# The first modulation by pairs of chunks, with four tiles of the first projection open at once

## What is computed

```
m = silu(cond) @ ada_w + ada_b          # cond: one row for context, one for latent tokens
shift, scale, ... = split(m, 6)         # six parts of 1024 columns; a second block has six more
h = rms_norm(x, norm1_g) * (1 + scale) + shift
z = h @ ab_w_in                         # 3088 columns; the first projection
qkv = silu(depthwise_conv3(z[qkv part]))   # 1536 columns, three taps along the tokens
```

## Time and profile before

| | |
|---|---|
| median of the runs | 1631.31 us |
| the profiled execution | 1633.56 us, its span 1631.7 us |
| TensorE busy | 1535.8 us (94%) |
| VectorE busy | 1126.5 us (69%) |
| ScalarE busy | 797.4 us (49%) |
| GpSimd busy | 122.9 us (8%) |
| data moved | 230.80 MB, 141 GB/s in the mean |

### The profile page before, as it was taken

The page is one execution under the profiler, slowest core; times in us unless marked ns, Lnnn a source line. Parts: engine busy times, 40 slices in busy tenths (PEclk is TensorE's granted clock), DMA queues, the critical chain, the costliest instruction groups (busy, mean ns, idle before and its releaser), DMA issues.

```text
span 1631.7 us, 31148 instructions
## 1 busy us (share of the span) xinstructions
PE 1535.8 (94%) x11566; PEld 1355.6 (83%) x11566; DVE 1126.5 (69%) x1853; ACT 797.4 (49%) x1437; POOL 122.9 (8%) x139
## 2 busy tenths in 40 slices
PE   5899988899899999999899999999999889999998
PEld 3688878787688888878786799999898669999997
DVE  5986866544798888887735478875666755577653
ACT  2545554243544545322445567765445455666542
POOL 2000052512000000010000010001000001000000
PEclk8999999899899999999899999999899999999999
DMA  9354520002244445566431045556454214255552
GB/s 368 108 180 164 186 66 2 3 2 78 94 177 170 165 166 179 174 213 217 173 110 52 5 151 190 183 197 214 144 168 143 84 59 143 92 191 182 186 188 90
DMA packets 62957, 230.80 MB, mean 141 GB/s; under 512 B 6800, under 2 KB 8080, under 8 KB 62352
## 3 DMA queue, kind: packets, MB, share of 16 engines
q1 hardware_dynamic: 61408, 223.37, 39.5%
q0 software_dynamic: 1168, 5.80, 1.0%
q10 hardware_dynamic: 288, 0.33, 0.1%
HBM read 228.43 MB, written 1.05 MB: 141 GB/s over the span
## 4 chain that ended last, share of the span: by engine, by line
PE 85%; DVE 8%; ACT 4%; issue 2%; DMA 1%; POOL 1%; DVEq 0%; ACTq 0%; POOLq 0%
PE proj L662 23%; PE proj L663 23%; PE proj L664 23%; PE bank L714 1%; PE bank L925 1%; DVE w_low L2165 1%; ACT w_high L1647 1%; PE proj L1145 1%; DMA ident_sb<-ident 1%; PE bank L942 1%; PE bank L972 1%; POOL tmp L1516 1%; PE proj L1147 1%; PE proj L1146 1%; PE bank L1160 1%
## 5 line engine op out<-in xcount | busy, mean ns | idle before, releaser
L662 PE MATMUL proj<-h_high,w_high 128*128 128x256 f32 (+1 forms) x1776 | 583.0, 328 | 19.9 <-DVE h_low L2198 13.5
L663 PE MATMUL proj<-h_low,w_high 128*128 128x256 f32 (+1 forms) x1776 | 572.0, 322 | 0.0
L664 PE MATMUL proj<-h_high,w_low 128*128 128x256 f32 (+1 forms) x1776 | 570.6, 321 | 0.0
L2165 DVE TENSOR_TENSOR w_low<-w_raw,w_high 128x1024 fp32r<-128x1024 f32 x322 | 393.3, 1224 | 152.9 <-ACT w_high L1647 151.5
L1647 ACT ACTIVATE w_high<-w_raw 128x1024 fp32r<-128x1024 f32 x322 | 337.9, 1054 | 232.0 <-PE proj L664 228.0
L662 PEld LDWEIGHTS proj<-h_high,w_high 128*128 128x128 f32 x1776 | 337.2, 190 | 56.5 <-issue 18.4
L664 PEld LDWEIGHTS proj<-h_high,w_low 128*128 128x128 f32 x1776 | 337.8, 190 | 27.2
L663 PEld LDWEIGHTS proj<-h_low,w_high 128*128 128x128 f32 x1776 | 337.5, 190 | 24.4
L662 PE MATMUL proj<-act_high,w_high 128*128 128x256 f32 (+1 forms) x608 | 190.6, 313 | 0.1
L663 PE MATMUL proj<-act_low,w_high 128*128 128x256 f32 (+1 forms) x608 | 189.7, 312 | 0.0
L664 PE MATMUL proj<-act_high,w_low 128*128 128x256 f32 (+1 forms) x608 | 189.3, 311 | 0.0
(11 more groups left out here) (413 smaller groups left out, 1911.2 us busy)
## 6 DMA issues: line engine op xcount, KB each, us to landing
w_raw<-w_stream SPq DMA_DIRECT2D x322, 512.0 KB, 3.3
a_ring<-a_stream SPq DMA_DIRECT2D x80, 512.0 KB, 4.1
a_first<-a_head SPq DMA_DIRECT2D x4, 1024.0 KB, 18.0
a_first<-a_stream SPq DMA_DIRECT2D x4, 1024.0 KB, 18.6
x<-x_in SPq DMA_DIRECT2D x1, 2048.0 KB, 10.3
late_tab<-late_tables POOLq DMA_DIRECT2D x1, 1408.0 KB, 6.6
cond_rows<-cond_rows SPq DMA_DIRECT2D x1, 1024.0 KB, 5.6
cond_rows<-cond_rows POOLq DMA_DIRECT2D x1, 1024.0 KB, 5.1
```

Source lines behind the costliest of these rows:

```text
L662: mm(out_, wh, xh, start=first, stop=False)
L663: mm(out_, wh, xl, start=False, stop=False)
L664: return mm(out_, wl, xh, start=False, stop=last)
L2165: v.tensor_tensor(wl(n), RAW[:, n % 4, :], wh(n), ALU.subtract).then_inc(w_low, 1)
```

## The change

The shifts are made in pairs of chunks. `a_head` is stored so that a load of 1 MB holds the columns of two chunks for all 1024 inputs, and TensorE takes the weights as the stationary operand and the two conditions as two moving columns (`front_shift`), so the result lies on partitions at once. The repeated condition `CB0` is no longer loaded: TensorE spreads it with the identity and VectorE copies it (four copies). VectorE's row sums, small operations and chunks are cut in pairs likewise (`front_sums`, `front_modulation`, `front_chunks`). GpSimd's early additions of squares go, and TensorE sums all 8 chunks. Four tiles are open at once: tiles 0 and 1 in `proj`, 2 and 3 in banks 2 and 3, with two more buffers of each half of the weights. The blocks of `ada_w` pass through rings (5 row buffers, 3 column buffers) rather than lying side by side. The table of columns and the identity now stand first in SyncE's queue. `mod_tile` no longer runs beside tiles 0 to 3; four more of them run beside tiles 12 to 17 (`IN_MODS`).

```diff
+FRONT = 4
+ROW_RING = 5
+COL_RING = 3
-        "a_head": moving(a["ada_w"][0][:, :A_COLS * P]),
+        "a_head": column_pairs(a["ada_w"][0][:, :A_COLS * P]),
         # TensorE
+            def front_shift(g, some=(0, 1)):
+                for c in some:
+                    if c == 0:
+                        pe.wait_ge(a_cols[g % COL_RING], 16 * (g // COL_RING + 1))
+                        if g >= 2:
+                            pe.wait_ge(mod_front, g - 1)
+                    for k in range(KC):
+                        at = k % 4 * 256 + c * P
+                        last = mm(SHIFTS[g % 2][:, 2 * c:2 * c + 2], ACOL[:, g % COL_RING, k // 4, at:at + P], SC[:, 2 * k:2 * k + 2], start=(k == 0), stop=(k == KC - 1))
+                    if c == 1:
+                        last.then_inc(shifted, 1)
+            def front(j, *chunks):
+                for k in chunks:
+                    if k == 0:
+                        weights(j)
+                        if j < 2:
+                            free_bank(j)
+                    pe.wait_ge(n_lo, NORM_S0["n1_0"] + k + 1)
+                    w = slice(k * P, (k + 1) * P)
+                    last = mm3(first_bank(j)[:], wh(j)[:, w], wl(j)[:, w], HH[:, k, :], HL[:, k, :], k == 0, k == KC - 1)
+                    if k == KC - 1:
+                        last.then_inc(pe_done, 1)
+            for s in range(2):
+                for h in range(2):
+                    for k in range(4):
+                        c = 2 * (4 * h + k) + s
+                        last = mm(BK[1 + 2 * s + h][:, k * P:(k + 1) * P], SC[:, c:c + 1].to_broadcast([P, P]), ID[:], start=True, stop=True)
+                    last.then_inc(cond_spread, 1)
...
+            pe.wait_ge(cond_ready, 2)
+            norm_sum("n1_0")
+            front_shift(0, (0,))
+            norm_spread("n1_0")
+            front_shift(0, (1,))
+            front_shift(1)
+            front(0, 0, 1)
+            front(1, 0, 1)
+            front_shift(2)
+            front(0, 2, 3)
+            front(1, 2, 3)
+            front_shift(3)
+            front(2, 0, 1, 2, 3)
+            front(0, 4, 5)
+            front(1, 4, 5)
+            front(2, 4, 5)
+            front(3, 0, 1, 2, 3, 4, 5)
+            front(0, 6)
+            front(1, 6)
+            for j in range(2):
+                front(j, 7)
+            for j in range(2, FRONT):
+                front(j, 6, 7)
         # ScalarE
             for t in range(GATES):
-                split(t + 2)
+                if t < 2 or t >= FRONT:
+                    split(t + FRONT if t < 2 else t + 2)
                 conv_in(t, t, 0, COL_AT["bconv"], T2)
         # VectorE
+            front_sums(0)
+            front_sums(1)
+            front_sums(2)
+            norm_factor("n1_0")
+            low(0)
+            dve.wait_ge(n_bc, 1)
+            front_modulation(0)
+            front_chunks(0)
+            low(1)
+            front_sums(3)
+            front_modulation(1)
+            front_chunks(1)
+            front_sums(4)
+            low(2)
+            front_sums(5)
+            front_modulation(2)
+            front_chunks(2)
+            low(3)
+            front_sums(6)
+            front_sums(7)
+            front_modulation(3)
+            front_chunks(3)
+            for t in range(FRONT):
+                if t < 2:
+                    low(t + FRONT)
+                conv(t, t, 0, COL_AT["bconv"], T2)
...
         # GpSimd
-            sum_early("n1_0")
```

More of the change, by code:

```diff
@@ L329, in two_blocks_kernel @@
         zone = cursor[0]
[L331 to L334, removed]
         cursor[0] = tmp_at
@@ L514, in two_blocks_kernel @@
         a_landed = [sem(f"a_landed{i}") for i in range(2)]
[L516 to L519, removed]
+        w_high, w_low, pe_done, tile_out = map(sem, ("w_high_ready", "w_low_ready", "pe_done", "tile_out"))
+        cond_ready, mod_ready, init, m_acc = map(sem, ("cond_ready", "mod_ready", "init", "m_acc"))
+        rows_in = sem("rows_in")
         n_sq, n_early, n_ss, n_root, n_std, n_bc, n_xn, n_hi, n_lo = map(sem, ("n_sq", "n_early", "n_ss", "n_root", "n_std", "n_bc", "n_xn", "n_hi", "n_lo"))
@@ L727, in norm @@
                 norm_spread(name)
-            pe.wait_ge(init, 1)
[L731 to L742, removed]
@@ L758, in lengths @@
                 last.then_inc(G["l2_ss"], 1)
-            for t in range(4, GATES):
+            for t in range(FRONT, GATES):
                 tile(t, t, slice(0, T2), T2)
@@ L1445, in _ @@
+            load_row(0)
+            load_row(1)
             load_cols(0)
-            load_rows(0)
+            load_row(2)
+            load_w(0)
             load_cols(1)
-            load_rows(1)
-            load_rows(2)
+            load_w(1)
+            load_row(3)
+            load_row(4)
             load_cols(2)
-            load_rows(3)
+            load_w(2)
+            load_row(5)
+            load_row(6)
             load_cols(3)
-            for n in range(4):
-                load_w(n)
+            load_w(3)
@@ L1455, in _ @@
+            load_row(7)
             load_a(0)
             load_a(1)
-            with sp.Fori(0, 5) as i:
+            for s in range(FRONT):
+                next_w(s)
+            with sp.Fori(0, 2) as i:
                 for s in range(4):
-                    next_w(s, 4 * i)
+                    next_w(s + FRONT, 4 * i)
                     load_a(s + 2, 4 * i)
-            for s in range(20, 25):
+            for s in range(GATES, 25):
                 next_w(s)
-                if s < 22:
-                    load_a(s + 2)
+                for j in IN_MODS.get(s, ()):
+                    if j + 2 < MOD_IN:
+                        load_a(j + 2)
@@ L2281, in _ @@
+            for s in range(2):
+                for h in range(2):
+                    dve.wait_ge(cond_spread, 2 * s + h + 1)
+                    ins = v.tensor_copy(CB0[:, s, h * 512:(h + 1) * 512], BK[1 + 2 * s + h][:])
+            ins.then_inc(cond_ready, 1)
+            dve.wait_ge(cond_ready, 2)
+            dve.wait_ge(m_acc, 2)
+            front_sums(0)
+            front_sums(1)
+            front_sums(2)
+            norm_factor("n1_0")
             low(0)
+            dve.wait_ge(n_bc, 1)
```

144 lines of the change are left out of this document (81 added, 63 removed).

## The result

The changed kernel takes 1646.81 us (median of 4 runs, 1643.44 to 1648.46) beside 1632.36 us for the kernel before on the same chip: ratio 1.009, 95% interval 1.007 to 1.011, so 14.5 us slower. The profiled execution took 1646.14 us around a span of 1644.0, 12.3 us more span than before.

The account below looks back on a forecast made before the run. TensorE's projections bound the kernel, except at the start. Tile 6 at 92.0 instead of 85.7 us is 6.3, plus 2.8 for the restart: 9.1 us slower, median 1631.31 to 1640.4 us; likeliest 1636 to 1645, whole range 1624 to 1647.

Parts of the forecast that it names:

- Direction and the start: Kernel start up to tile 6: slower, with tile 6 starting at 92.0 us, 9.1 us lost including the restart.
- Loads: First transfers: table and identity there at 4.1 us, x at 9.0, the condition spread and copied by 11.7.
- The norm's sum: First norm on TensorE: 64 one-column instructions from 11.7 to 23.1 us, 11.4 us, clock falling 2.6 us in.
- Shifts: TensorE's two-column products: 7.0 us per pair of chunks at half clock; first ready at 31.9 us, second at 38.9.
- VectorE's ledger: VectorE's row sums, w_low and chunk pairs at the start: 32.6 us from 31.9, last pair done at 64.5.
- Bursts: TensorE's 12 products between shifts: 4.2 us each, shifts 4.4; tile 0 ends at 71.0 us, TensorE the bound.
- Four tiles at once: Tiles 0 to 3 end together: ScalarE needs 21.0 us until tile 6, TensorE idles 4.8, restart loses 2.8.
- Moved behind: Four modulation tiles moved to tiles 12 to 17 fit VectorE's idle time: 0 us, at most 9.8.
- The rest of the span: Behind tile 6's start both kernels run the same code at TensorE's pace, so no further difference.
- The clock: TensorE at the start: one-column runs don't hold the clock up; 0.50 from about 15 to 42 us.
- Rival 1: Clock stays full through sum and shifts: tile 0 ends at 56.5 us, 5.4 us faster, 1625.9 us; chance 0.22.

Follow-up runs that it names:

- a2: Changed kernel with the four moved modulation tiles beside tiles 5, 7, 9 and 11 and one beside each tile from 12 on; 1639.37 us.
- a1: Changed kernel with ScalarE's splits of blocks 6, 7 and 8, and their w_low, each one tile earlier; 1645.99 us.
- b1: Changed kernel with splits of blocks 6, 7 and 8 one tile earlier and tiles 6 and 7 in banks 2 and 3; 1637.63 us.
- c3: Changed kernel with the same modulation load from tile 12 on in another order: three tiles beside tile 12, two beside 13, one each beside 14 to 18; 1641.90 us.
- a4: Kernel before with only its modulation tiles moved as in the change; 1636.21 us beside 1632.49 us for the kernel before.
- b2: Changed kernel with only the first norm's sum made with 128 moving columns, shifts keeping two; 1635.22 us.
- a3: Changed kernel with 128 moving columns per instruction in the first norm's sum and the shifts, extra results unread; 1629.78 us.
- c2: Kernel before with the sums of seven norms made with 128 moving columns instead of one; 1626.57 us beside 1630.93 us for the kernel before.
- c1: Changed kernel with GpSimd's early additions of squares put back, so TensorE sums three chunks in 24 one-column instructions; 1647.11 us.

## Why the prediction was right and where it failed

- **Direction and the start: right.** The forecast was 9.1 us by tile 6; it was 10.0 when the tiles are in step again.
- **Loads: two errors that cancel.** The table and the identity took 2.6 us from issue to landing and not 3.3, so both were there at 3.8 us instead of 4.1 and the spread was done at 10.1, but x landed at 11.0 instead of 9.0. The sum began at 11.78 instead of 11.7, released by the squares and not by the copies: the right time by luck.
- **The norm's sum: mis-sized.** 13.5 us, not 11.4. The clock fell at its start (0.53 in 12 to 14 us) and not 2.6 us in. In the other runs with this narrow sum it fell 0.8 us in (a2), 1.1 (a1) and 1.7 (b1 and c3), in all of them before the 2.6. An idle stretch of 1.0 to 1.6 us stood in front of each; in front of the runs of the earlier trace rows there was none at 848.63 and one of 0.50 us at 1148.37. Whether the idle stretch brings the fall forward is not shown.
- **Shifts: right.** 3.41, 1.92 and 10.03 us against 3.5, 1.8 and 10.5. The first is ready at about 33.9 instead of 31.9, all of it from the sum.
- **VectorE's ledger: right by luck.** Its fourth pair is done at 64.5 us (62.83 + 1.68), as forecast, but it began 1.9 us later than forecast and took 30.7 us instead of 32.6. The forecast counted 1.22 us for each row sum and each w_low; they follow one another at 1.15 us.
- **Bursts: between the two lines.** Tile 0 ends at 73.9, forecast 71.0. Of the 2.9 us, 1.7 came in with the second shift (done at 40.6 instead of 38.9). The bursts took 5.3 and 4.4 us against 4.2 each, the shifts between them 3.66 and 4.30 against 4.4, and the dense work behind them was mostly at 1.2 GHz until 62 us (0.54 in 56 to 62).
- **Four tiles at once: right in size, short of a cause.** 20.3 us to tile 6 against 21.0, a wait of 4.27 against 4.8, a restart of 1.6 against 2.8 (tile 6's 24 products took 7.07 us and not 5.5). The bank of tile 4 was a second condition that I had not seen (a1).
- **Moved behind: this step failed.** It said that the modulation tiles fit, since VectorE was busy 11.95 of 20 us, and put 0, with 9.8 as the bound. It is 5.1 us (3.0 of waits, the rest the low clock behind them), and the kernel before pays 5.2 for it alone (a4). Load was the wrong question: VectorE had the time (16.34 of 20 us now), but two small results for which TensorE waits in order stand behind a second tile (c3).
- **The rest of the span** gave 2.6 us back in this execution, for the most part by low stretches of the clock that moved. No row of before could have told it. The 9.1 us of the forecast became 10.0 + 5.1 - 2.6 = 12.5 us between the profiles; the medians stand 1.9 us further apart (14.5), as the profiled execution before was 1.2 us above its median and that after 0.7 us below.
- **The clock: right.** That the clock falls in these narrow products with TensorE busy is shown by b2, where 64 instructions with 128 columns passed at full clock up to 18.7 us and those with two had lost it by 24 us, without a gap between them. Rival 1, with the clock up, was nearly built by a3: it put tile 0's end at 56.5 and tile 6 at 77.5; a3 has 58.0 and 78.3. Its time was 1625.9, and a3 took 1629.8, 3.9 us more; the moved tiles cost a3 3.5 us (5.1, less the 1.6 that it gains on the changed kernel there).

The Trainium skill, "TensorE: Matmul & The Clock Gate", section "What's actually happening", lets the clock follow how busy TensorE has been. By the profile's count of busy time b2's shifts, 6.00 of 6.00 us at 1.2 GHz, disagree with that.

## What to carry to other kernels

An instruction with one or two moving columns costs almost as much as one with 128 (0.11 against 0.115 to 0.13 us at full clock), and behind the long runs of them here the wide work began at half clock: try such runs with more columns, even if nobody reads them. It gave 17.0 us in the changed kernel and 4.4 in the one before. When work moves to an engine with idle time, ask not only for the idle share but which small result stands behind the new place, and whether another engine waits for it in its own order. A wait that names one releaser can hide a second condition that comes true shortly before; list all conditions of the waiting instruction before moving one.

## What the runs showed of the hardware

- 64 instructions of 128x128 against 128x128 took 7.38 us at full clock (b2), 64 with one column 13.49 us at half (the changed kernel). With the wide ones a low clock also came back, between 15 and 16 us in a3 and near 30 us in c2, where in the narrow ones of the kernel before it did not.
- In c1 TensorE stood still for 12.56 us, the clock fell within that stretch (0.96 in 12 to 14 us, 0.50 behind), and its first narrow products ran at half clock, 24 in 5.25 us; after the wait of the kernel before, 2.44 us, 24 took 5.25 us too.
- The same 64 instructions of the first sum took 12.19, 12.82, 13.09 and 13.49 us (b1, a1, a2, the changed kernel), since the clock fell 1.7, 1.1, 0.8 and 0.3 us in; what stands behind moves with them.
- A wait of 1.2 us for `g_tok` was followed by a fall of the clock in the changed kernel (0.64 in 168 to 172 us), in a4 and in c1, and by none in a1, a3, b1 and b2. What decides it is not shown.
